# Part of the modulation product on VectorE, and a fourth early home for its weights

## The reference

```python
sc = jax.nn.silu(c)
scc = jax.nn.silu(c_ctx)
shift, scale, gate = jnp.split(sc @ w_ada[l] + b_ada[l], 3, axis=-1)
shift_c, scale_c, gate_c = jnp.split(scc @ w_ada[l] + b_ada[l], 3, axis=-1)
hc = _rmsnorm(ctx, g_pre[l]) * (1.0 + scale_c) + shift_c
hx = _rmsnorm(x, g_pre[l]) * (1.0 + scale[:, None]) + shift[:, None]
zx = hx @ w_in[l]
```

## Time and profile before

| | us |
|---|---|
| median of 3 runs | 2030.25 (2030.2 to 2035.45) |
| the profiled execution, device time | 2031.12 |
| its span in the profile | 2029.3 |
| TensorE busy in the span | 1956.6 |
| VectorE busy in the span | 1196.0 |
| ScalarE busy in the span | 998.8 |

### The profile page before, as it was taken

The page is one execution under the profiler, slowest core; times in us unless marked ns, Lnnn a source line. Parts: engine busy times, 40 slices in busy tenths (PEclk is TensorE's granted clock), DMA queues, the critical chain, the costliest instruction groups (busy, mean ns, idle before and its releaser), DMA issues.

```text
span 2029.3 us, 28189 instructions
## 1 busy us (share of the span) xinstructions
PE 1956.6 (96%) x10681; PEld 1662.2 (82%) x10681; DVE 1196.0 (59%) x1631; ACT 998.8 (49%) x1454; POOL 98.2 (5%) x115
## 2 busy tenths in 40 slices
PE   4998999989999999999998999999999999999999
PEld 2657888888888888878888998788889999998887
DVE  2235655576558887767875675656655444444554
ACT  4434222235555666654436434466544555656642
POOL 1000000000013344000000000000000000000000
PEclk9999999999999999999998999999999999999999
DMA  9983322238656666649874544444565655555564
GB/s 309 349 253 104 95 82 85 83 114 246 187 180 187 180 174 185 187 149 360 313 246 137 156 145 146 145 125 135 172 192 172 182 165 164 163 163 160 167 187 161
DMA packets 210025, 360.41 MB, mean 178 GB/s; under 512 B 14248, under 2 KB 61760, under 8 KB 209008
## 3 DMA queue, kind: packets, MB, share of 16 engines
q1 hardware_dynamic: 200432, 349.36, 55.9%
q10 hardware_dynamic: 8848, 8.47, 1.7%
q0 software_dynamic: 624, 0.92, 0.2%
HBM read 356.55 MB, written 2.16 MB: 177 GB/s over the span
## 4 chain that ended last, share of the span: by engine, by line
PE 87%; DVE 4%; DMA 2%; ACT 1%; issue 1%; POOL 1%; SPq 0%; ACTq 0%; POOLq 0%; DVEq 0%
PE acc L635 49%; PE acc L622 15%; PE acc L603 11%; DMA ex_a<-acs_scratch 1%; PE side L993 1%; PE side L603 1%; DVE w_lo L1824 1%; PE side L862 1%; DVE conv L1982 1%; PE side L758 1%; PE side L854 1%; PE side L1022 1%; PE side L685 1%; DMA raw_first<-in_w_ada 1%; PE side L1130 1%
## 5 line engine op out<-in xcount | busy, mean ns | idle before, releaser
L1824 DVE TENSOR_TENSOR w_lo<-raw,w_hi 128x1024 fp32r<-128x1024 f32 (+2 forms) x560 | 678.1, 1217 | 491.9 <-ACT w_hi L1194 485.5
L1194 ACT CAST w_hi<-raw 128x1024 fp32r<-128x1024 f32 (+1 forms) x544 | 560.0, 1036 | 602.2 <-PE acc L635 407.1
L635 PE MATMUL acc<-w_hi,h_hi 128*128 128x512 f32 (+1 forms) x1312 | 526.2, 401 | 6.4 <-DVE w_lo L1824 6.4
L635 PE MATMUL acc<-w_hi,h_lo 128*128 128x512 f32 (+1 forms) x1312 | 510.8, 389 | 0.0
L635 PE MATMUL acc<-w_lo,h_hi 128*128 128x512 f32 (+1 forms) x1312 | 509.3, 388 | 0.0
L635 PEld LDWEIGHTS acc<-w_hi,h_hi 128*128 128x128 f32 x1312 | 247.8, 189 | 55.1 <-issue 3.8
L635 PEld LDWEIGHTS acc<-w_hi,h_lo 128*128 128x128 f32 x1312 | 247.2, 188 | 52.7
L635 PEld LDWEIGHTS acc<-w_lo,h_hi 128*128 128x128 f32 x1312 | 248.1, 189 | 46.7
L622 PE MATMUL acc<-h_hi,w_hi 128*128 128x256 f32 x896 | 259.1, 289 | 7.6 <-DVE w_lo L1824 6.5
L622 PE MATMUL acc<-h_lo,w_hi 128*128 128x256 f32 x896 | 255.3, 285 | 0.0
L622 PE MATMUL acc<-h_hi,w_lo 128*128 128x256 f32 x896 | 255.2, 285 | 0.0
(11 more groups left out here) (383 smaller groups left out, 2046.4 us busy)
## 6 DMA issues: line engine op xcount, KB each, us to landing
raw<-in_w_in SPq DMA_DIRECT2D x184, 512.0 KB, 4.3
raw<-in_w_in_odd SPq DMA_DIRECT2D x128, 512.0 KB, 3.8
raw<-in_w_in_even SPq DMA_DIRECT2D x96, 512.0 KB, 3.7
raw<-in_w_out SPq DMA_DIRECT2D x64, 512.0 KB, 6.1
raw_first<-in_w_ada SPq DMA_DIRECT2D x58, 512.0 KB, 8.7
gate_w<-in_w_ada SPq DMA_DIRECT2D x32, 512.0 KB, 6.7
raw<-in_w_out_even SPq DMA_DIRECT2D x32, 512.0 KB, 4.7
raw<-in_w_out_odd SPq DMA_DIRECT2D x32, 512.0 KB, 3.9
```

The source lines that it names most:

```text
L635: o = nc.tensor.matmul(ACC[b][:, 0:n], l, r, start=first and kk == 0 and m == 0, stop=last and kk == 1 and m == 2)
L1194: act.copy(WHI[:, u % 4, :, 0:n], RAW[:, u % 4, :, 0:n]).then_inc(hi_ready, 1)
L1824: dve.tensor_tensor(WLO[:, u % 4, :, 0:n], RAW[:, u % 4, :, 0:n], WHI[:, u % 4, :, 0:n].bitcast(F32), ALU.subtract).then_inc(lo_ready, 1)
```

## The change

In rounds 1 to 7 six of the sixteen row blocks, all of v=0 and the first two of v=1, are no longer multiplied on TensorE. VectorE multiplies each with its element of the vector and sums them (`ada_mac`) into `MACC`, one row of 512 per vector. TensorE takes v=2, v=3 and the other half of v=1, in that order, and then adds the two sums over partitions with the one-columns `ONEC` in column groups 0 and 1, after a wait for VectorE (`mac_used`). `ada_used` now counts three loads a round. A home with blocks of VectorE is freed by `mac_used` too. VectorE's queue has the blocks of the next round in front of the low part and `mod`, and the rest of them in front of the halves; `ada_out` moves behind the halves. The first four loads have early homes (`RAW4`), the six homes of `RAW6` are taken in turn from n=4 on, and the wait for the turns stands before n=7.

```diff
--- before.py
+++ after.py
@@ -123,14 +123,32 @@
 VEC_AT = 14
 
 
+MACS = 6
+
+
 def ada_slot(n):
 
-    return n if n < 6 else 3 + n % 3 if n % 6 < 3 else n % 3
+    return n if n < 4 else (n - 1) % 6
+
+
+def ada_sem(n):
+
+    return 6 if n == 3 else ada_slot(n)
 
 
 def ada_uses(n):
 
-    return len([m for m in range(n + 1) if ada_slot(m) == ada_slot(n)])
+    return len([m for m in range(n + 1) if ada_sem(m) == ada_sem(n)])
+
+
+def ada_by_pe(e, v):
+
+    return AW4 + 3 * (e - 1) + (v - 1 or 3) if e else v + 1
+
+
+def ada_macs(e, v):
+
+    return 2 * (e - 1) + v + 1 if e and v < 2 else 0
 
 
 GATE_BEAT = [11 + 3 * n // 2 for n in range(32)]
@@ -227,8 +245,8 @@
 
     RAW = at("raw", 0, [P, 4, 2, NCOL])
     RAW6 = at("raw_first", 136, [P, 6, 4, 2, 256])
-    RAW3 = at("raw_early", 48, [P, 3, 4, 2, 256])
-    ada_raw = lambda n: (RAW3 if n < 3 else RAW6)[:, ada_slot(n)]
+    RAW4 = at("raw_early", 48, [P, 4, 4, 2, 256])
+    ada_raw = lambda n: (RAW4 if n < 4 else RAW6)[:, ada_slot(n)]
     WHI = at("w_hi", 16, [P, 4, 2, NCOL], F32R)
     WLO = at("w_lo", 32, [P, 4, 2, NCOL], F32R)
 
@@ -256,6 +274,8 @@
     JUNK = at("junk", 112, [P, D])
     ADR = at("ada_rows", 120, [P, 2, NCOL])
     SEA = at("pick_sum", 124, [P, 2])
+    ONEC = at("one_col", 124.5, [P, 2, 32])
+    MACC = at("ada_macs", 112, [P, 2, 2, NCOL])
     SC = at("c_wide", 190, [P, KT, 32])
     VR = at("vec_rows", 184, [P, 4, P])
     HF = at("h_f", 186, [P, 2, 2 * SEQ])
@@ -356,7 +376,8 @@
         sc_ok, xt_act, xt_dve = sem("sc_ok"), sem("xt_act"), sem("xt_dve")
         gate_in, gate_used, gsum_done = [sem(f"gate_in{x}") for x in range(3)], sem("gate_used"), sem("gsum_done")
         raw_in = [sem(f"raw_in{s}") for s in range(4)]
-        ada_in, ada_used, hh_ok = [sem(f"ada_in{s}") for s in range(6)], sem("ada_used"), sem("hh_ok")
+        ada_in, ada_used, hh_ok = [sem(f"ada_in{s}") for s in range(7)], sem("ada_used"), sem("hh_ok")
+        onec_ok, mac_used, mac_done = sem("onec_ok"), sem("mac_used"), sem("mac_done")
         hi_ready, lo_ready, unit_used = sem("hi_ready"), sem("lo_ready"), sem("unit_used")
         acc_done = [sem(f"acc_done{b}") for b in range(3)]
         acc_free = [sem(f"acc_free{b}") for b in range(4)]
@@ -477,16 +498,18 @@
             for kind, e, u in LOADS:
                 if kind == "ada":
                     n = AW4 * e + u
-                    if n == 9:
+                    if n == 7:
                         sp.wait_ge(turned, KT)
-                    elif 6 <= n < 9:
-                        sp.wait_ge(ada_used, n - 2)
-                    elif n >= 12:
-                        sp.wait_ge(ada_used, n - 5)
+                    elif n >= 10:
+                        e0, v0 = divmod(n - 6, AW4)
+                        if v0:
+                            sp.wait_ge(ada_used, ada_by_pe(e0, v0))
+                        if ada_macs(e0, v0):
+                            sp.wait_ge(mac_used, ada_macs(e0, v0))
                     for h in range(2):
                         sp.dma_start(ada_raw(n)[:, :, h, :],
                                      w_of["w_ada"][:, 4 * u:4 * u + 4, h * D + e * 256:h * D + e * 256 + 256]
-                                     ).then_inc(ada_in[ada_slot(n)], 16)
+                                     ).then_inc(ada_in[ada_sem(n)], 16)
                 else:
                     k = u // 2 * 2
                     if u >= 4:
@@ -678,13 +701,28 @@
             def ada(e, v):
 
                 n = AW4 * e + v
-                if v == 0 and e:
+                def strips(n, kts, first, last):
+
+                    pe.wait_ge(ada_in[ada_sem(n)], ada_uses(n) * 32)
+                    for j in kts:
+                        o = nc.tensor.matmul(SB[3][32 * j:32 * j + 32, :], SC[:, 4 * (n % AW4) + j, :], ada_raw(n)[:, j],
+                                             start=first, stop=last, tile_position=(0, 32 * j))
+                    o.then_inc(ada_used, 1)
+
+                if e == 0:
+                    strips(n, range(4), v == 0, v == AW4 - 1)
+                elif v == 2:
                     pe.wait_ge(mod_ok, e)
-                pe.wait_ge(ada_in[ada_slot(n)], ada_uses(n) * 32)
-                for j in range(4):
-                    o = nc.tensor.matmul(SB[3][32 * j:32 * j + 32, :], SC[:, 4 * v + j, :], ada_raw(n)[:, j],
-                                         start=v == 0, stop=v == AW4 - 1, tile_position=(0, 32 * j))
-                o.then_inc(ada_used, 1)
+                    strips(n, range(4), True, False)
+                elif v == 3:
+                    strips(n, range(4), False, False)
+                    strips(n - 2, range(MACS - 4, 4), False, True)
+                    pe.wait_ge(onec_ok, 1)
+                    pe.wait_ge(mac_used, ada_macs(e, 1))
+                    for j in range(MACS - 4):
+                        o = nc.tensor.matmul(SB[3][32 * j:32 * j + 32, :], ONEC[:, j, :], MACC[:, e % 2, j, :],
+                                             start=False, stop=True, tile_position=(0, 32 * j))
+                    o.then_inc(mac_done, 1)
 
             def ada_turn(e):
 
@@ -1826,13 +1864,18 @@
 
             dve.sem_inc(gate_free, 2)
             dve.memset(SC[:, :, 2:32], 0.0).then_inc(sc_ok, 1)
+            seq(dve.memset(ONEC[:], 0.0))
+            dve.memset(ONEC[:, 0, 0:1], 1.0)
+            dve.memset(ONEC[:, 1, 1:2], 1.0).then_inc(onec_ok, 1)
             dve.wait_ge(con_in, 48)
             pick = con("ident").rearrange("p (j s) -> p s j", s=32)[:, 0:2, :]
             dve.tensor_reduce(SEA[:], pick, AX.X, ALU.add).then_inc(sc_ok, 1)
 
             def ada_out(e):
 
-                dve.wait_ge(ada_used, AW4 * e + AW4)
+                dve.wait_ge(ada_used, ada_by_pe(e, 1 if e else AW4 - 1))
+                if e:
+                    dve.wait_ge(mac_done, e)
                 if e >= 2:
                     dve.wait_ge(ada_done, e - 1)
                 dve.tensor_copy(ADR[:, e % 2, :], SB[3][:]).then_inc(ada_ok, 1)
@@ -1854,6 +1897,27 @@
                     o = dve.scalar_tensor_tensor(MOD[:, s, k], ADAV[:, 16 + 2 * e:18 + 2 * e, s], 1.0,
                                                  vec("g_pre", 2 * e, 2), ALU.add, ALU.mult)
                 o.then_inc(mod_ok, 1)
+
+            def ada_mac(e, i0, i1):
+
+                for i in range(i0, i1):
+                    n = AW4 * e + i // 4
+                    if i % 4 == 0:
+                        dve.wait_ge(ada_in[ada_sem(n)], ada_uses(n) * 32)
+                    if i == 0 and e >= 3:
+                        dve.wait_ge(mac_done, e - 2)
+                    w = ada_raw(n)[:, i % 4]
+                    for s, name in enumerate(("c", "c_ctx")):
+                        acc = MACC[:, e % 2, s, :].rearrange("p (h n) -> p h n", h=2)
+                        if i == 0:
+                            o = dve.tensor_scalar(acc, w, vec(name, i), None, ALU.mult)
+                        else:
+                            o = dve.scalar_tensor_tensor(acc, w, vec(name, i), acc, ALU.mult, ALU.add)
+                    if i in (3, MACS - 1):
+                        o.then_inc(mac_used, 1)
+                        dve.wait_ge(mac_used, ada_macs(e, i // 4))
+                    else:
+                        seq(o)
 
             def xt_out(kt):
 
@@ -1938,22 +2002,30 @@
             def first_lo(m):
                 lo(m // UPC, m % UPC, 320 if m % 2 else NCOL)
 
+            ada_mac(1, 0, 1)
             halve(0)
             halve(1)
             first_lo(0)
             first_lo(1)
+            ada_mac(1, 1, MACS)
             ada_out(1)
+            ada_mac(2, 0, 2)
             mod(1)
             first_lo(2)
+            ada_mac(2, 2, MACS)
             halve(2)
             halve(3)
             ada_out(2)
+            ada_mac(3, 0, 2)
             mod(2)
             for e in range(3, UPC):
                 first_lo(2 * e - 3)
-                ada_out(e)
+                ada_mac(e, 2, MACS)
                 halve(2 * e - 2)
                 halve(2 * e - 1)
+                ada_out(e)
+                if e + 1 < UPC:
+                    ada_mac(e + 1, 0, 2)
                 first_lo(2 * e - 2)
                 mod(e)
             first_lo(13)
@@ -2617,7 +2689,7 @@
         def _(pool):
             vec_load(pool, VEC_TILES[1:], 1, "rest", vec_in)
             vec_load(pool, VEC_TILES[:1], 0, "rest", vec_in)
-            pool.wait_ge(ada_used, 28)
+            pool.wait_ge(ada_used, ada_by_pe(6, 3))
             pool.dma_start(CON[:, P:], dram["const_a"][:, P:]).then_inc(bc_in, 16)
             pool.dma_start(BCS[:, 0:64], dram["dt_bias"].rearrange("o d h -> (o d h)").partition_broadcast(P)).then_inc(bc_in, 16)
             pool.dma_start(BCS[:, 64:128], dram["a_log"].rearrange("o d h -> (o d h)").partition_broadcast(P)).then_inc(bc_in, 16)
```

## The result

The changed kernel takes 2036.22 us (median of 20 runs, 2031.2 to 2040.5), the kernel before 2031.99 (20 runs, 2030.04 to 2035.45). The forecast was +3.3 (2033.5, with a range of 2027.5 to 2039), inside 0.3% with a chance of 0.78. The profiled execution took 2036.86 us, its span is 2035.1 (2029.3 before).

What follows compares the result with a forecast made beforehand. TensorE and transfers were both full, transfers stricter, the 32nd load ending the stage. Terms gave +1.2 without the clock's fall, +3.5 to +3.9 with it; +3.3 was taken, 2034.4 profiled, 2033.5 median, range 2027.5 to 2039.

Steps and rivals of the forecast that it cites:

- The stage is ended by the last load: Modulation rounds: landing of the 32nd w_ada load (n=31) ends the stage; the change is worth its shift of the prefix end.
- TensorE's round is 13.4: Steady rounds: two strip pairs run in the time of one, so the period falls from 14.29 to 13.4 us.
- VectorE: Steady rounds: blocks add 8.2 us to 4.2, sum 12.4, under 13.4 and 14.4, so VectorE holds nobody up.
- The stops at n=7, n=10 and n=11: Early load stream: three dry stops lose 1.9, 2.3 and 1.8 us, 6.0 against 4.7 before; stream 1.3 later.
- Rounds 2 and 3: Start-up: TensorE waits 4.2 and 3.7 us for VectorE's blocks; round 4 starts at 95.3, 7.3 late.
- The tail: End of round 7: strips of v=1 and the sums follow v=3, adding one pass of 0.87 us before the copy.
- the late landing of the last load: Last w_ada load: 1.3 us from the stream and about 0.5 from a later slot, landing at 140.1 against 138.3.
- if TensorE is late, 2 more: Bound on the load stream: 2 us of further delay beyond the 1.3 if TensorE is late.
- the fall of the clock: Units 2 and 3 after the new waits: slow clock costs 2.3 and perhaps 1.7 us; sum +3.5 to +3.9, without it +1.2.
- Rival A: The loads win: n=10's stop and n=11's don't occur, stream 2.8 us earlier, 3.5 faster, 2026.8; chance 0.17.
- Rival B: Strip pairs run one after the other, or VectorE's blocks take 1.6: round 14.2, 6 to 9 slower, 2038; chance 0.18.
- Rival C: Everything hides: VectorE and TensorE catch up, clock doesn't fall, tail is one pass; within 1 us, 2030.5; chance 0.10.

Runs made afterwards that it cites:

- early home alone: Kernel before with only the fourth early home and the new order of homes, all row blocks on TensorE: ratio 0.9993.
- blocks from round 3: Changed kernel with VectorE's six blocks only in rounds 3 to 7, earlier rounds all on TensorE: ratio 0.9993 to the kernel before.
- blocks from round 4: Changed kernel with VectorE's six blocks only in rounds 4 to 7, rounds 1 to 3 all on TensorE: ratio 1.0000 to the kernel before.
- four blocks: Changed kernel with four blocks a round on VectorE in place of six, v=1 whole on TensorE: ratio 1.0002 to the kernel before.
- blocks from round 2: Changed kernel with VectorE's six blocks only in rounds 2 to 7, round 1 all on TensorE: ratio 1.0023 to the kernel before.

## Why the prediction was right

Direction and size were right, +4.3 us (3.1 to 5.7) against +3.3, though the size partly by luck (the last load, below). The absolute time, 2036.2 against 2033.5, is off by more, because the kernel before had a median of 2030.25 in the three runs shown and of 2031.99 in all its runs. Point by point:

- *The stage is ended by the last load.* Shown: 138.3 to 144.1 for the landing, 5.1 for the end of the prefix; and taking 0.75 MB from ahead of the last loads gave 5.3 us to the kernel before.
- *TensorE's round is 13.4.* 13.44 and 13.45. The two pairs run together.
- *VectorE.* Blocks 2 to 5 took 5.76 us (5.8), ten multiply-adds 7.21; all added work 55.3 us where 7 x 8.2 = 57 was worked out.
- *The stops at n=7, n=10 and n=11.* Issued at 38.4, 50.8 and 56.4, as worked out (38.3, 51.1, near 56). n=11 landed at 62.2, 1.9 later than before (1.3 expected).
- *Rounds 2 and 3.* Waits of 4.12 and 3.72 (4.2 and 3.7); the clock at 0.50 after the first and 0.63 on the mean after the second; round 4 at 99.6 (95.3 at full clock, 99.3 with both falls).
- *The tail.* From the start of v=3 to the copy 2.08 us against 1.13: +0.95 (0.87). Unit 11 and its columns took 4.24 us at full clock, as hoped.
- *What was mis-sized* is one term: the late landing of the last load. I had 1.3 us for the stream and 0.5 for later homes, 140.1 (some 2 us more if the clock fell); it is 144.1. Against the kernel before, the landings are 1.9 us late at n=11, 3.7 at n=20, 4.8 at n=23, 5.5 at n=28 and 5.8 at n=31. The homes of n=8, n=9, n=12 and n=13 come free only with the blocks of rounds 2 and 3: n=18 was issued 6.6 us behind n=17 (83.3 against 76.7), and the low part 4 that frees a home for `w_in` came at 91.7. So the stream lost a second time, in 80 to 100 us (308 and 291 GB/s), which the prediction had only as a bound ("if TensorE is late, 2 more"). n=23 was then held by TensorE itself: it was issued at 102.4, when v=1 of the late round 4 was done.
- *Why the size still came near.* The sum without the fall of the clock and with the landing as measured gives the columns of round 7 at 146.3 + 4.0 = 150.3, and they came at 150.26. The forecast came near because I took the case with the fall of the clock for another 2.3 us. That fall happened, but round 7 found TensorE waiting 1.26 us for n=30 even so; the loads brought what the fall was counted for. So the size is right partly by a wrong term, and that is luck. That the fall costs nothing is shown for round 3 only; it also made round 4 late, and what that gave to the loads is not separated.
- *Small slips of the working*, which change nothing: 46.5 + 3 x 1.5 is 51.0 and not 51.1, the wait from 64.8 to 69.1 is 4.3 and not 4.2, 24 matmuls at 0.23 us are 5.5 and not 5.6. And TensorE did have short gaps after 46 us: it was busy for 8.06 us of 60 to 70 in the kernel before.
- *Rival A* (the loads win): its premise failed at the place named, n=10 at 50.8 and not by 48.8. Even alone, the home gave only 1.4. *Rival B*: the pairs do not run one after the other. *Rival C*: the waits don't all hide; it is nearly what the versions from rounds 3 and 4 and with four blocks do.

How far the loss is TensorE's waits in rounds 2 and 3, and how far the homes that VectorE frees late, was separated only in part: blocks from round 3 on cost nothing, from round 2 on about 5 us, and filling most of the waits with work did not change the time (1.0019 against 1.0021).

## What to carry to other kernels

When an engine and a stream of loads are both full, ask first which of the two lands the last item of the stage; work taken off the other is worth nothing, and the cheapest gain is to move bytes that nobody needs yet behind that item (one number here, 5.3 us). Before a second engine is made a consumer of a shared ring of buffers, write down when it frees each of the first few homes: a steady state that fits (12.4 us of work in 14.4) does not help if the first rounds have nothing else to overlap with, and it should begin in the round whose order gives it cover. And it is worth trying to put no instruction that waits for a load ahead of one that the critical engine waits for; the waits of 0.9 to 1.7 us above suggest it, but no run here has the other order.

## What was not expected of the hardware

- A dry stream cost more than the 1.9 us assumed from the first window, and not the same each time: from the landing of n=5 to that of n=9, the ten profiles with the stop at n=7 lost 2.4 to 4.2 us of transfer (3.8 with the early home alone, 2.7 in the changed kernel).
- GpSimd's four small loads of 0.75 MB (2.1 us at 350 GB/s) cost the last load 3.8 us (138.3 against 134.5) and the kernel 5.3, of which 1.5 are the clock that then fell in round 7.
- The same code after the prefix took from 1862.3 (four blocks) to 1867.5 us (blocks from round 4) in the profiled executions; the kernel before took 1864.0. In 168 to 174 us, after the wait of 3.07 to 3.08 us that all versions have there, the granted clock was 1.00 in the kernel before and 0.64 and 0.65 in the versions from rounds 4 and 3. A difference of 2 us in the prefix can vanish in this.
- A wait of 3.72 us at the same place left the clock at 0.51 in one profile (blocks from round 3) and at 1.00 in another (blocks from round 2), so the fall did not follow each such wait.
